# Around a mixture-of-experts loop: two blocks gathered ahead instead of three, adds moved to VectorE, own weights copied first, hidden layers turned in their own body, four tiles of sums loaded ahead

## What is computed

```python
def moe(x, router_w, router_bias, wg, wu, wd, swg, swu, swd):
    scores = sigmoid(xt @ router_w)                  # 64 experts, 8 groups of 8
    ...                                              # best 4 groups, best 8 experts per token
    gates = ...                                      # weights of the 8, normalised, times 2.5
    h = silu(einsum('td,edf->tef', xt, wg)) * einsum('td,edf->tef', xt, wu)   # f = 128
    routed = einsum('tef,efd->td', h * gates[..., None], wd)
    shared = (silu(xt @ swg) * (xt @ swu)) @ swd     # 256 wide
    return routed + shared
# then x = x + g2 * moe(norm(x)), and a final RMS norm of every row
```

## Time and profile before

| what | us |
|---|---|
| median of 3 runs | 1601.85 (1600.15 to 1602.02) |
| the profiled execution | 1599.84 |
| its span in the profile | 1598.0 |
| TensorE busy in the span | 1504.7 (94%) |
| VectorE, ScalarE, GpSimd busy | 719.7, 530.2, 541.5 |
| data moved by DMA | 301.66 MB, mean 189 GB/s |
| expert loop, first gate/up product to last regular down | 913.70 to 1519.99 |

### The profile page before, as it was taken

The page is one execution under the profiler, slowest core; times in us unless marked ns, Lnnn a source line. Parts: engine busy times, 40 slices in busy tenths (PEclk is TensorE's granted clock), DMA queues, the critical chain, the costliest instruction groups (busy, mean ns, idle before and its releaser), DMA issues. The chain is left out here.

```text
span 1598.0 us, 28991 instructions
## 1 busy us (share of the span) xinstructions
PE 1504.7 (94%) x9259; PEld 925.4 (58%) x9260; DVE 719.7 (45%) x1463; ACT 530.2 (33%) x1255; POOL 541.5 (34%) x605
## 2 busy tenths in 40 slices
PE   6999999999979999999899799999999999999977
PEld 2554678787847775555455455555555555555523
DVE  2400053333446662688753344444344444444438
ACT  2400066343056561211200034333333333333312
POOL 0001135333163311111055445455545555445410
PEclk8999999999979999999999899999999999999979
DMA  9991002010093108102000599999999999996589
GB/s 347 338 362 41 20 1 54 18 41 20 2 372 111 55 1 341 40 40 105 14 1 0 215 297 335 311 340 340 337 338 340 335 326 317 267 276 129 83 264 378
DMA packets 108677, 301.66 MB, mean 189 GB/s; under 512 B 13020, under 2 KB 24112, under 8 KB 107836
## 3 DMA queue, kind: packets, MB, share of 16 engines
q1 hardware_dynamic: 82686, 216.81, 35.9%
q0 software_dynamic: 25920, 83.91, 21.8%
HBM read 230.26 MB, written 80.90 MB: 195 GB/s over the span
## 5 line engine op out<-in xcount | busy, mean ns | idle before, releaser
L2186 PE MATMUL ps_g<-w_exp,mix 128*64 x1408 | 324.0, 383 | 6.7 <-DVE own_gu L2308 2.8
L2189 PE MATMUL ps_g<-own_gu,mix 128*64 128x256 f32 x1408 | 324.1, 383 | 0.0
L2133 POOL DMA_INDIRECT sum_rows<-mix,scatter_row x88 | 175.2, 1991 | 237.8 <-DVE mix L2245 219.0
L2186 PEld LDWEIGHTS ps_g<-w_exp,mix 128*64 128x64 f32 x1408 | 186.2, 137 | 107.2 <-issue 9.9
L2189 PEld LDWEIGHTS ps_g<-own_gu,mix 128*64 128x64 f32 x1408 | 186.2, 137 | 0.0
L2158 PE MATMUL ps_y<-w_exp,hidT 128*64 x352 | 171.6, 610 | 2.4 <-ACT own_d L2258 2.4
L2159 PE MATMUL ps_y<-own_d,hidT 128*64 128x512 f32 x352 | 171.6, 610 | 0.0
L511 PE MATMUL ps_f<-late,hT 128*128 128x256 f32 x624 | 145.3, 390 | 0.0
L2308 DVE COPY own_gu<-w_exp 128x2048 f32 x89 | 109.7, 1233 | 58.9 <-issue 43.6
L511 PEld LDWEIGHTS ps_f<-late,hT 128*128 128x128 f32 x624 | 120.2, 196 | 18.8 <-issue 1.9
L2245 DVE COPY mix<-ps_y 128x512 f32<-128x512 f32 x88 | 60.8, 691 | 112.8 <-PE ps_y L2159 112.8
(11 more groups left out here) (352 smaller groups left out, 2610.4 us busy)
## 6 DMA issues: line engine op xcount, KB each, us to landing
w_exp<-in_exp_w_gate SPq DMA_DIRECT2D x64, 512.0 KB, 5.9
w_exp<-in_exp_w_up SPq DMA_DIRECT2D x64, 512.0 KB, 6.7
w_exp<-in_exp_w_down SPq DMA_DIRECT2D x64, 512.0 KB, 7.5
sum_rows<-mix SPq DMA_DIRECT2D x10, 2048.0 KB, 18.4
w_exp<-sum_rows SPq DMA_DIRECT2D x36, 512.0 KB, 13.7
ada_ring<-in_w_ada SPq DMA_DIRECT2D x8, 2048.0 KB, 11.0
wring<-in_w_ada SPq DMA_DIRECT2D x3, 2048.0 KB, 13.0
h_rows<-h SPq DMA_DIRECT2D x9, 512.0 KB, 2.6
```

Of the source, the lines that this page charges most:

```text
L2133: pool.indirect_dma_start(out=dram["y"][k % 2], out_offset=bass.IndirectOffsetOnAxis(ap=si[k][:], axis=0), in_=y[k], in_offset=None, bound ...
L2186: pe.matmul(ps_g[par][0:HALF, 0:2 * FF].rearrange("p (k f) -> p k f", k=2), xT[par][:, j * P:j * P + HALF], w[:, bass.ds(slot * 3, 2), ff] ...
L2189: last = pe.matmul(ps_g[par][HALF:P, 0:2 * FF].rearrange("p (k f) -> p k f", k=2), xT[par][:, j * P + HALF:(j + 1) * P], own_gu[par][:, :, ...
```

## The change

Six edits. `X_EARLY` becomes 2: GpSimd gathers two blocks in the old stage and blocks 2 and 3 at the start of the new one. GpSimd no longer adds tile 7 of the shared expert; VectorE adds tiles 7 and 8, each right behind its product. At the start of the expert stage VectorE copies the own gate and up weights of block 0 before its half of the turned x instead of after it. TensorE turns the hidden layer of block b at the end of b's own body instead of at the start of the next. SP and VectorE work with four tiles ahead (`FIRST = 4`), TensorE keeps three (`OPEN = 3`).

```diff
--- before.py
+++ after.py
@@ -1323,7 +1323,8 @@
 SUM_ROWS = T + P
 NOWHERE = 1 << 20
 NW = 8
-W_EARLY = X_EARLY = 3
+W_EARLY = 3
+X_EARLY = 2
 
 
 def out_and_route(nc, dram, keep):
@@ -1725,7 +1726,6 @@
             pool.wait_ge(h2_out[1], 16 * 4)
             for k in range(X_EARLY):
                 gather(k)
-            add_shared(NT - 2)
             pool.wait_ge(first_x, 16 * X_EARLY)
 
         @block.vector
@@ -1928,10 +1928,10 @@
             keep_shared(NT - 3)
             hidden(NT - 1)
             write_table()
-            keep_shared(NT - 2)
-            keep_shared(NT - 1)
-            dve.wait_ge(t_done, NT)
-            dve.tensor_tensor(keep["x1"][:, NT - 1, :], keep["x1"][:, NT - 1, :], t6[(NT - 1) % 2], ALU.add)
+            for t in (NT - 2, NT - 1):
+                keep_shared(t)
+                dve.wait_ge(t_done, t + 1)
+                dve.tensor_tensor(keep["x1"][:, t, :], keep["x1"][:, t, :], t6[t % 2], ALU.add)
 
 
 def expert_weights(dram):
@@ -1979,7 +1979,8 @@
         H = D // 2
         NS = 4
         NB = 3 * NW // NS
-        FIRST = 3
+        FIRST = 4
+        OPEN = 3
         sums = w[:].rearrange("p (t s) n -> p t s n", s=NS)
         r = [own_gu[0][:, i, :] for i in range(2)]
         junk, fg = own_gu[1][:, 0, :], own_gu[1][:, 1, :]
@@ -2108,7 +2109,8 @@
                                         in_offset=bass.IndirectOffsetOnAxis(ap=gi[k][:], axis=0),
                                         bounds_check=T - 1, oob_is_err=False).then_inc(x_in[k], 16)
 
-            gather(X_EARLY, X_EARLY)
+            for k in range(X_EARLY, 4):
+                gather(k, k)
 
             def body(i):
                 for k in range(4):
@@ -2172,8 +2174,6 @@
                     b, par = i * 4 + k, k % 2
                     e = expert_of(pe, b, 0)
                     slot = e % NW
-                    if not (first(i) and k == 0):
-                        turn_h(1 - par, b - 1)
                     pe.wait_ge(w_ready, e + 1)
                     pe.wait_ge(own_gu_done, b + 1)
                     pe.wait_ge(xT_act, b + 1)
@@ -2198,11 +2198,11 @@
                             pe.wait_ge(y_act, b - 1)
                             pe.wait_ge(y_dve, b - 1)
                         down(1 - par, b - 1, former % NW)
+                    turn_h(par, b)
                     former = e
 
             last, _ = fours(pe, body)
             slot = expert_of(pe, last, 0) % NW
-            turn_h(1, last)
             pe.wait_ge(y_act, last)
             pe.wait_ge(y_dve, last)
             down(1, last, slot)
@@ -2213,10 +2213,10 @@
                     pe.wait_ge(sum_in[t % NB][i], 16 * (t // NB + 1))
                     pe.matmul(ps_low[t % 3], keep["ident"][:], sums[:, t % NB, i, 0:H], start=(i == 0), stop=False)
 
-            for t in range(FIRST):
+            for t in range(OPEN):
                 add_early(t)
             for t in range(NT):
-                if t >= FIRST:
+                if t >= OPEN:
 
                     pe.wait_ge(g_done, 2 * (t - 2))
                     add_early(t)
@@ -2297,8 +2297,6 @@
 
         @block.vector
         def _(dve):
-            move_x(dve, dve.tensor_copy, xT_dve, 1, 0, 0, False)
-
             def own_gate_up(par, b, wait):
 
                 e = expert_of(dve, b, 1)
@@ -2308,6 +2306,7 @@
                 dve.tensor_copy(own_gu[par][:], w[:, bass.ds((e % NW) * 3, 2), :]).then_inc(own_gu_done, 1)
 
             own_gate_up(0, 0, False)
+            move_x(dve, dve.tensor_copy, xT_dve, 1, 0, 0, False)
 
             def body(i):
                 for k in range(4):
```

## The result

The changed kernel takes 1612.67 us (median of 5 runs, 1611.49 to 1616.23), the kernel before 1602.02 us on the same chip (5 runs, 1600.15 to 1604.62): ratio 1.0068, 95% interval 1.0052 to 1.0084. The forecast was 1609, slower: 7 us on the median, where it came to 10.65. The profiled execution has a span of 1611.2 us, against 1598.0.

What follows compares the result with a forecast made beforehand. TensorE was taken to bound the expert loop, DMA engines close behind. Terms summed to +8.9 us at the loop's end, -0.7 after it: +8.2, from the median 1601.85 to 1610.0, given as 1609; range 1599 to 1615.

Steps and rivals of the forecast that it cites:

- The stage change: Start of expert stage: with two gathers the last lands at 905.3 instead of 907.1; gain 1.8 us, bounds 0 and 2.6.
- The first copies: Before the first gate/up: copying own weights ahead of the x half starts TensorE earlier; gain 1.0 us, bounds 0.5 and 1.2.
- The half clock: First expert block: an earlier start puts more of it at half clock; 0.2 us lost, bounds 0.3 less to 1.4 more.
- The boundaries: Every fourth block: branch and loads start behind the wait; 0.1 first, 14 x 0.55 = 7.7, six late 5.5 us lost.
- The weights' stall: Loop, 1144 to 1162 us: weights land late, TensorE loses 1.9 us; 1.8 of it to go, bounds 1.4 and 1.9.
- rival B: Late loop boundaries: slow register loads become quick when shifted, so +1.5 us, 1602.5, no change; chance 0.18.
- rival A: Loop boundaries: the wait does not stop TensorE's stream, so they cost nothing; -3.5 us, 1598, faster; chance 0.13.
- Exit: Loop exit: the last hidden is turned at once, ScalarE copies during the exit; gain 1.3 us, bounds 0.8 and 2.5.
- First sum: Last stage: two more loads stand ahead in SP's queue, so the sums start 1.4 us later, bounds 0 and 2.6.
- The sums: Last stage: VectorE's pair of tile 3 moves ahead of the chain that VectorE bounds; gain 0.8 us.
- C: Loop: weight stall not absorbed, start wins nothing because the clock stays at half longer; +12.4 us, 1613.5; chance 0.07.
- D: Stage change wins 2.6 instead of 1.8 us, four tiles ahead cost nothing; +6.0 us, 1607; chance 0.62 together with the forecast.

Runs made afterwards that it cites:

- the experiment: The changed kernel with VectorE's two copies ahead of the loop in the former order: 4.81 us from first turn to gate/up instead of 4.12; one run, 1611.43 us.
- the last kernel above: The changed kernel with three tiles ahead, norm's weights early and the former expert's load behind the turn of x, own-body turn kept: 1601.87 us, ratio 0.9991.

## Why the prediction was right

**The stage change.** Predicted 1.8 us gained, measured 1.56. The reading held: VectorE's last add takes 1.22 us instead of 3.41 and ends at 906.58, the second gather, issued at 902.27 and landing 5.3 us later, decides. It is issued 1.83 us ahead of the product's row, as before the change; the landing took 0.1 us more than the 5.2 I had taken, and from the landing to the first turn it is 2.0 us where the earlier trace rows have 1.9. From the last gather's issue to the first turn it is 6.8 to 7.3 us in all fourteen profiles, while VectorE ends anywhere from 2.3 to 5.5 us ahead of the turn: it is the last gather that decides.

**The first copies.** Predicted 1.0 gained, measured 0.61, and 0.7 by the experiment. Two terms were off: SP's second issue took 0.51 us, so that the copy started 1.60 us behind the stage's first matmul and not 1.35, and the copy took 1.47 us beside a gather's issue, where I had the 1.23 of the earlier trace rows. The half clock was the worse miss: 1.06 us lost in this profile, 0.2 predicted. My bound was 1.4, but I took a value near no change without a row that spoke for it. The change isn't shown to be the cause, though. In the kernels with the former expert's load late and with three tiles this stretch is the same code, and there the copy took 1.23 us, gate/up came 3.7 us behind the first turn (the whole 1.0 gained), the clock was full 2.7 and 2.8 us behind that gate/up, and the first block took 7.14 and 7.18 us. The other eight profiles with the new start have 8.2 to 8.7 us, the three with three gathers 7.2. The term thus varies from one execution to the next by 1.5 us, and one profile can't price it.

**The boundaries.** This was the body of the forecast, +11.5 us for the loop, and it measured +11.9. By its terms: the first boundary 0.1 predicted, 0.13 measured. Early ones 0.55 predicted, 0.49 to 0.64 measured, 0.57 on average. Late ones: 6.0 us predicted for seven (0.55 for b = 63, which showed no hole, and 0.92 for each of the other six), 4.5 measured (8.20 against 3.74): the excess grew by 0.9 and 1.2 at b = 59 and 63, by 0.2 at 67 and 71, and by 0.6 to 0.7 at 75, 79 and 83; how slow a load is at a given place is what varies. The weights' stall: 1.8 predicted to vanish, 1.7 vanished (2.17 at b = 34 and 35 before, 0.49 after, with a boundary's price in it). Not predicted: 2.0 us of excess inside bodies, 1.7 in seven late blocks and 0.3 in block 13, where I had written "nothing is lost" and had named longer blocks as a sign of being wrong. There one slow load, 1.3 to 1.6 us, is enough to use up the slack of a single load. My sum took the slow loads over as they were, and rival B made them quick; in fact more of them were slow with the moved wait. That the two misses cancel is luck, and the loop's total is nearer to the forecast than its terms are.

**Does the wait stop the stream?** Yes, at all 21 boundaries: the stream's next instruction, of the loop's branch, starts 0.05 us after hidden is ready, where the earlier trace rows show it 0.9 us ahead. The same 0.05 us stands behind every other wait for hidden in the changed kernel, 87 in all. The kernel before has it too at 62 of the 65 waits inside bodies, so its trace had far more to say for this than the one place of the earlier trace rows. The picture in the Trainium skill (page "Perfetto Trace Analysis", section on the Tensor Engine Instruction), by which the sequencer is free once a matmul is in the wait queue, doesn't describe this; rival A fell with it, and the pair with the load moved by one place is the proof.

**Exit and last stage.** Exit 1.3 predicted, 1.37 measured, and the stream is the bound there ("issue", 3.50 us), not ScalarE. First sum 1.4 later predicted, 1.75 measured, but by two terms that partly offset each other: with the own-body turn the fourth tile costs 2.7 us, twice what I had and just beyond my bound of 2.6, and with three tiles this way is 1.4 us shorter with the own-body turn than without it (19.1 against 20.6), which I hadn't in the sum and can't explain. The sums were to gain 0.8 us and gained 0.13: the pair did leave VectorE's chain, but a wait of 0.6 us for the norm's weights is there in its place. The prediction counted the loads ahead of the first tiles' and forgot that the four extra loads of the fourth tile stand ahead of the norm's weights too.

**The rivals.** A (1598) is excluded. B (the late loads become quick, 1602.5) fits two boundaries of seven at most. C (the stall stays, the clock is lost, 1613.5) is the nearest of all by its number, and right on the clock of this profile, but wrong on the stall, which went: the number is met by other terms. D (the gather wins 2.6, part 4 costs nothing) is out with 1.56 and 1.75. Of the 2.9 us that separate the sum from the trace, the half clock is 0.9, the end of the sums 0.7, and the copy, the gather, the first sum's way and the loop the rest.

**Open.** What makes register loads slow isn't settled. Where TensorE's load took 1503 ns, at 1459.1 us, VectorE's and ScalarE's of the same table took 305 and 278 ns at 1461.4 and 1461.5, so it isn't the table's memory as such. The place of the wait has a part in it (8.8 us in slow loads before, 20.6 after), but how isn't shown.

## What to carry to other kernels

A wait in TensorE's stream is a barrier for everything written behind it, loads of registers and branches of a loop included. So ask of a moved wait not what the array does in order, but what the stream still has to fetch behind it, and how much shadow it has: put the loads of the next step ahead of the wait, or behind a long run of matmuls. A hole of half a microsecond at every fourth block costs more than all that was won around the loop, and what is won ahead of a bound stage may be taken back by a transfer that the stage then reaches too early. And before a loss in one profile is put down to a change, look at the same stretch in every profile that has the same code there.

## What the runs showed of the hardware

- One register load, mostly of 0.31 to 0.38 us, added behind a wait, made a boundary 0.92 us longer on average, since the register operations and the assertion around it are in order too (two successive loads start 0.8 us apart); ahead of the wait it cost nothing.
- Register loads on TensorE's queue took 0.30 to 0.35 us in most of the loop. In its last third loads of up to 1.0 to 1.5 us turned up in the five kernels without own-body turns, and more of them, up to 1.6, in the nine with own-body turns; those also had one of 1.6 to 1.7 us near 933 us and one of 1.3 to 1.6 near 1010.
- A gather's issue on GpSimd took 1.80 us instead of 1.05 while VectorE added two SBUF tiles, and VectorE's 128x2048 copy 1.47 instead of 1.21 us beside a gather's issue. The Trainium skill (page "SBUF — State Buffer", section "SBUF: two separate sides") has the two engines share a port pair that one holds for a whole instruction; the trace agrees as far as the gather's issue is slowed by an add that began before it, and the copy by an issue that began before it.
- Behind three of six holes of 2.3 us in the loop the granted clock fell (0.64 over the next four us), and the next block was 1.7 us longer; behind the other three, and behind the hole of 1.3 us at 1476.6, it stayed at 1.00. In the last kernel above it fell behind one of 1.6 us at b = 35; behind one of 1.6 there in the kernel with the former expert's load late it did not.
- A stretch of 900 us of nearly the same code differed by up to 6 us between profiled executions (901.9 to 908.3), more than most effects looked for here. From the first turn of the expert stage to gate/up of block 1 the same code took 10.8 to 13.1 us.
